# Scatters of expert outputs in two halves, and ranks dealt over 16 groups of partitions, in a hybrid SSD/attention/MoE layer

## What is computed

```
grp_logits = x @ w_rg + b_rg;  g_star = argmax(grp_logits)          # 4 groups
sel = (x @ w_re + b_re)[group g_star]                               # 8 experts in it
top_val, top_idx = top_k(sel, 2);  w2 = softmax(top_val) * p_g
expert_id = g_star * 8 + top_idx                                    # 32 experts in all
out = x + sum over the token's 2 experts of w2 * down(silu(gate(x)) * up(x))
```

## Time and profile before

| | |
|---|---|
| median of three runs | 737.94 us (736.9 to 739.18) |
| the profiled execution's own time | 737.7 us |
| its span, first to last instruction | 736.1 us |
| granted TensorE clock over the span | 0.975 |
| PE busy | 688.6 us (94%) |
| DVE, ACT, POOL busy | 384.5, 290.2, 153.3 us |
| DMA moved | 156.99 MB, mean 213 GB/s |

### The profile page before, as it was taken

How to read it: one execution, slowest core, us unless ns; L and a number is a source line. 1 busy time by engine, 2 the same in 40 slices (tenths; PEclk the granted TensorE clock), 3 DMA queues, 4 the chain that set the end, 5 groups by cost and what they waited for, 6 DMA issues and landing times.

```text
span 736.1 us, 10543 instructions
## 1 busy us (share of the span) xinstructions
PE 688.6 (94%) x3780; PEld 470.3 (64%) x3780; DVE 384.5 (52%) x850; ACT 290.2 (39%) x655; POOL 153.3 (21%) x179
## 2 busy tenths in 40 slices
PE   6999999999999999999989999989999977879984
PEld 5878788788787887666656688876543332324442
DVE  6865787876868724766787653462222211212211
ACT  5934542655455535745565432321121211112200
POOL 2300010231412101312241242001113241111321
PEclk9999999999999999999999999987999998989999
DMA  8333323333323043290020049698999999999994
GB/s 292 90 113 115 102 76 113 114 115 100 114 73 115 15 128 116 83 346 1 28 88 2 1 167 421 288 358 303 408 417 414 407 408 398 423 418 417 412 400 129
DMA packets 48454, 156.99 MB, mean 213 GB/s; under 512 B 13768, under 2 KB 13924, under 8 KB 36112
## 3 DMA queue, kind: packets, MB, share of 16 engines
q1 hardware_dynamic: 40640, 140.97, 50.2%
q0 software_dynamic: 6880, 9.02, 4.2%
q10 hardware_dynamic: 880, 6.30, 2.2%
HBM read 154.00 MB, written 18.19 MB: 234 GB/s over the span
## 4 chain that ended last, share of the span: by engine, by line
PE 70%; SPq 14%; DMA 7%; DVE 4%; issue 2%; ACT 2%; DVEq 0%; POOLq 0%; POOL 0%; ACTq 0%
PE bank L1291 14%; PE bank L1293 14%; PE bank L1292 14%; SPq L394 6%; PE bank L1672 5%; DMA s_gu<-in_w_expert_gate_dram 4%; SPq L422 4%; SPq L408 4%; PE bank L1481 3%; PE bank L1504 3%; PE bank L1490 3%; PE bank L1701 2%; PE bank L1645 2%; PE bank L1396 2%; PE bank L1629 1%
## 5 line engine op out<-in xcount | busy, mean ns | idle before, releaser
L277 DVE TENSOR_TENSOR s_wl<-s_raw,s_wh 128x512 fp32r<-128x512 f32 x105 | 89.3, 893 | 26.6 <-ACT s_wh L947 26.3
L1672 PE MATMUL bank<-s_gu,s_xgT 128*64 128x512 f32 x352 | 82.9, 626 | 17.0 <-DMA s_gu<-in_w_expert_up_dram 17.0
L947 ACT ACTIVATE s_wh<-s_raw 128x512 fp32r<-128x512 f32 x120 | 73.6, 628 | 38.5 <-PE bank L1293 18.0
L1291 PE MATMUL bank<-s_wh,s_hTh 128*128 128x512 f32 x192 | 78.9, 411 | 0.0
L1293 PE MATMUL bank<-s_wh,s_hTl 128*128 128x512 f32 x192 | 75.1, 391 | 0.0
L1292 PE MATMUL bank<-s_wl,s_hTh 128*128 128x512 f32 x192 | 74.8, 389 | 0.0
L1672 PEld LDWEIGHTS bank<-s_gu,s_xgT 128*64 128x64 f32 x352 | 27.9, 144 | 70.9 <-issue 70.9
L1213 ACT ACTIVATE s_sg<-bank,s_slot_scale 128x256 f32<-128x256 f32 x16 | 7.6, 474 | 149.5 <-PE bank L1672 112.3
L1701 PE MATMUL bank<-s_dn,s_hidT 128*64 128x512 f32 x256 | 60.4, 613 | 3.8 <-issue 1.9
L2241 DVE COPY s_hidT<-bank 128x256 f32<-128x256 f32 x16 | 6.8, 424 | 92.8 <-PE bank L1681 92.8
L2274 DVE SCALAR_TENSOR_TENSOR s_yrow<-bank,s_slot_scale,s_xg 128x512 f32<-128x512 f32 x30 | 21.1, 746 | 50.4 <-PE bank L1701 46.1
(11 more groups left out here) (303 smaller groups left out, 1402.2 us busy)
## 6 DMA issues: line engine op xcount, KB each, us to landing
s_gu<-in_w_expert_gate_dram SPq DMA_DIRECT2D x30, 1024.0 KB, 26.3
s_dn<-in_w_expert_down_dram SPq DMA_DIRECT2D x28, 1024.0 KB, 27.0
s_gu<-in_w_expert_up_dram SPq DMA_DIRECT2D x28, 1024.0 KB, 26.0
s_raw<-in_w_in_dram SPq DMA_DIRECT2D x88, 256.0 KB, 3.7
s_raw<-in_w_out_dram SPq DMA_DIRECT2D x32, 256.0 KB, 3.2
s_decay_rows<-decay_rows SPq DMA_DIRECT2D x4, 1024.0 KB, 4.7
s_xin<-in_x_dram SPq DMA_DIRECT2D x4, 512.0 KB, 5.8
s_zs<-in_x_dram SPq DMA_DIRECT2D x1, 2048.0 KB, 13.2
```

The costliest lines, as they stand in the source:

```text
L277: eng.tensor_tensor(low, full, high.bitcast(F32), ALU.subtract).then_inc(sem(f"{what}_low_{low_engine(what, i)}"), 1)
L947: act.activation(wh[:, i % HL, :], raw[:, i % RAW, :], ACT.Copy).then_inc(sem("w_high"), 1)
L1291: pe.matmul(dst, ah, bh, start=start, stop=False)
L1672: last = pe.matmul(ps[j][r, :].rearrange("p (w f) -> p w f", w=2), m["xgT"][:, j, k, r], gu[:, half, :, k, :], start=(k == 0), stop=(k == ...
```

## The change

- Each scatter of a pair p < 15 becomes two indirect DMAs, one for partitions 0 to 63 (the lower expert) and one for partitions 64 to 127 (the upper). Their semaphores count 32 a pair in place of 16. The gathers, the lone stores of L813, the gather of the last sums and the last pair's store stay whole.
- An index column is read from partition 0 on, so the upper half's indices are written once more into tables of 64 partitions (`first_far`, `second_far`, `slot_far`), by three small VectorE operations.
- TURN goes from 8 to 16: `rank_of` gives partition 4b + c the rank b + 16c (b of 16, c of 4). Sixteen consecutive ranks go to sixteen groups of four partitions.
- `turn` makes expert e start at rank 2 (e mod 8). The longest queue then ends at 56, still within 64.

```
-TURN = 8
+TURN = 16
...
+        first_far, second_far, slot_far = (sb(n, [CAP, NPAIR], I32) for n in ("first_far", "second_far", "slot_far"))
...
-            return rank_of[:, 0:CAP // 2].rearrange("p (b c) -> p c b", b=TURN)[:, 0:n // TURN, :]
+            return rank_of[:].rearrange("p (g b) -> p b g", g=TURN)[:, 0:n // TURN, :]
...
-            return 16 * sum(has_first(q) for q in range(p % 2, p + 1, 2))
+            return 32 * sum(has_first(q) for q in range(p % 2, p + 1, 2))
...
-            return 16 * sum(has_second(q) for q in range(p % 2, p + 1, 2))
+            return sum(32 if q < NPAIR - 1 else 16 for q in range(p % 2, p + 1, 2) if has_second(q))
...
-            pool.iota(rank_of[:], [[CAP // 2, 2], [1, TURN], [TURN, CAP // 2 // TURN]], ...)
+            pool.iota(rank_of[:], [[1, TURN], [TURN, CAP // TURN]], ...)
...
+            def half_rows(p, half, add):
+                near, far = (first_rows, first_far) if not add else (slot_rows, slot_far) if lone(p) else (second_rows, second_far)
+                return far[:, p:p + 1] if half else near[0:CAP, p:p + 1]
...
                 if has_first(p):
-                    pool.indirect_dma_start(out=out[:, :], ... ap=first_rows[:, p:p + 1] ..., in_=m["yrow"][:, j, :], ...)
+                    for half in range(2):
+                        r = slice(half * CAP, (half + 1) * CAP)
+                        pool.indirect_dma_start(out=out[:, :], ... ap=half_rows(p, half, False) ..., in_=m["yrow"][r, j, :], ...)
...
-                    pool.indirect_dma_start(out=out[:, :], ... ap=added_rows(p)[:, p:p + 1] ..., compute_op=ALU.add)
+                    for half in range(2):
+                        r = slice(half * CAP, (half + 1) * CAP)
+                        pool.indirect_dma_start(out=out[:, :], ... ap=half_rows(p, half, True) ..., in_=m["yrow"][r, j, :], ..., compute_op=ALU.add)
```

More of the change, by code:

```diff
@@ L663, in _ @@
                                pattern=[[1, P]], channel_multiplier=-1).then_inc(sem("consts"), 1)
-            pool.iota(rank_of[:], [[CAP // 2, 2], [1, TURN], [TURN, CAP // 2 // TURN]], base=0, channel_multiplier=0, allow_small_or_imprecise_dtypes=True)\
+            pool.iota(rank_of[:], [[1, TURN], [TURN, CAP // TURN]], base=0, channel_multiplier=0, allow_small_or_imprecise_dtypes=True)\
                 .then_inc(sem("pool_seq"), 1)
@@ L767, in _ @@
             lows(KC * 13 + HL, NSLOT)
-            pool.tensor_scalar(turn[:].rearrange("p (r v) -> p r v", v=TURN), counting(TURN).rearrange("p c b -> p (c b)").unsqueeze(1).broadcast_to([P, NE // TURN, TURN]),
-                               1.0 / P, None, ALU.mult).then_inc(sem("consts"), 1)
+            pool.tensor_scalar(turn[:].rearrange("p (r v) -> p r v", v=NEG), counting(TURN)[:, 0, 0:NEG].unsqueeze(1).broadcast_to([P, NG, NEG]),
+                               TURN / NEG / P, None, ALU.mult).then_inc(sem("consts"), 1)
             pool.wait_ge(sem("f_rstd"), TC)
@@ L832, in scatter @@
                 if has_first(p):
-                    pool.indirect_dma_start(out=out[:, :], out_offset=bass.IndirectOffsetOnAxis(ap=first_rows[:, p:p + 1], axis=0),
-                                            in_=m["yrow"][:, j, :], in_offset=None, bounds_check=T - 1, oob_is_err=False)\
-                        .then_inc(sem(f"first_out{j}"), 16)
+                    for half in range(2):
+                        r = slice(half * CAP, (half + 1) * CAP)
+                        pool.indirect_dma_start(out=out[:, :], out_offset=bass.IndirectOffsetOnAxis(ap=half_rows(p, half, False), axis=0),
+                                                in_=m["yrow"][r, j, :], in_offset=None, bounds_check=T - 1, oob_is_err=False)\
+                            .then_inc(sem(f"first_out{j}"), 16)
                 if p == NPAIR - 1:
@@ L844, in scatter @@
                     lone_landed(p)
-                    pool.indirect_dma_start(out=out[:, :], out_offset=bass.IndirectOffsetOnAxis(ap=added_rows(p)[:, p:p + 1], axis=0),
-                                            in_=m["yrow"][:, j, :], in_offset=None, bounds_check=T - 1, oob_is_err=False,
-                                            compute_op=ALU.add).then_inc(sem(f"second_out{j}"), 16)
+                    for half in range(2):
+                        r = slice(half * CAP, (half + 1) * CAP)
+                        pool.indirect_dma_start(out=out[:, :], out_offset=bass.IndirectOffsetOnAxis(ap=half_rows(p, half, True), axis=0),
+                                                in_=m["yrow"][r, j, :], in_offset=None, bounds_check=T - 1, oob_is_err=False,
+                                                compute_op=ALU.add).then_inc(sem(f"second_out{j}"), 16)
             def gather_last_sums():
@@ L2247, in rows_split @@
                 dve.tensor_scalar(first_away[:], ps[7][:, 0:NPAIR], 0.0, float(NO_ROW), ALU.is_lt, ALU.mult).then_inc(sem("dve_seq"), 1)
-                step()
-                step()
+                far = slice(CAP, 2 * CAP)
+                dve.tensor_scalar(first_far[:], ps[7][far, 0:NPAIR], float(NO_ROW), None, ALU.add).then_inc(sem("dve_seq"), 1)
+                dve.tensor_scalar(slot_far[:], ps[5][far, 0:NPAIR], float(NO_ROW), None, ALU.add).then_inc(sem("dve_seq"), 1)
+                for i in range(4):
+                    step()
+                dve.wait_ge(sem("dve_seq"), step())
+                dve.scalar_tensor_tensor(out=second_far[:], in0=ps[5][far, 0:NPAIR], scalar=float(NO_ROW), in1=first_away[far, :],
+                                         op0=ALU.add, op1=ALU.add).then_inc(sem("dve_seq"), 1)
                 dve.wait_ge(sem("dve_seq"), step())
```

## The result

The change makes the kernel slower: a median of 746.33 us (745.4 to 747.66) against 737.81 us, a ratio of 1.0119 (95% interval 1.0098 to 1.0141). The span of the profiled execution goes from 736.1 to 743.7 us.

The account below looks back on a forecast made before the run. The weight stream was taken to bound the kernel, with slow DMA engines lagging at the end. -1.3 + 0.95 - 0.5 = -0.85, + 0.1 gave about -0.8 us: 737.1 us against 737.94, range 734.8 to 740.0.

Parts of the forecast that it names:

- The bound and its place: From 575 us the weight stream limits; at the end, slow DMA engines lag by some 3.5 us from uneven rows.
- the first term of the sum: Balance of the scatters: halves spread evenly over 16 engines bring the end forward, -1.3 us, bounds 0 and -2.9.
- the sign of being wrong that I had named: At the end of the weight stream: forecast wrong if the weights' last landing moves by over 3 us.
- The fourth: Scatters: a half runs on only eight engines, slow ones lag 10 us or more, 748 us; chance 0.05.
- Rival 3: Weight stream, pairs 4 to 14: each store has its own engine price, adding 4.4 us, 741.5 us; chance 0.10.
- Rival 1: End of the kernel: balance counts in full, store landing backlog goes too, -2.7 us, 735.2 us; chance 0.19.
- Rival 2: End of the kernel: halves even nothing out, second half's later issue costs +0.95 to +1.3 us, 739.0; chance 0.18.
- What follows (VectorE, the last store, its landing) is unchanged: After the gather of the last sums: the rest of the program's end keeps its times, no cost added.
- POOL's issue: Store issue on POOL: halves take 0.65 and 1.0 us, a pair grows 1.3 us (0.6 to 3.2), hidden until pair 14.
- +0.95 - 0.5 = +0.45: Pair 14's stores to last gather: second half issued 0.95 us later, landing 0.5 us shorter with less lag.
- The small edits: VectorE's three operations, some 0.4 us before 519.7, hidden by idle time; rank tables and higher start free; completions 0.1 us.

Follow-up runs that it names:

- experiment 1: Changed kernel with halved stores kept, but the rank dealing and start ranks of the kernel before: 740.33 us, ratio 1.0043.
- experiment 2: Changed kernel with whole stores again, keeping the change's rank dealing and start ranks: 737.84 us, ratio 1.0013.
- experiment 5: Against experiment 1, halved stores kept, ranks 0 to 31 put in even partitions and 32 to 63 in odd ones: 738.01 us, ratio 1.0015.
- experiment 4: Kernel before, whole stores, with rank r put in partition r: 741.87 us, ratio 1.0063.
- experiment 10: Kernel before, whole stores, with ranks 0 to 31 in even partitions and 32 to 63 in odd ones: 741.67 us, ratio 1.0051.
- experiment 3: Against experiment 1, halved stores kept, with rank r put in partition r: 742.19 us, ratio 1.0064.

## Why the prediction was wrong

**The bound and its place: right.** The stage from 575 us is bound by the weight stream, it is the slowest engine that counts, and the lag at the end follows from the rows' spread over engines. Between the lines of the table the last weight packet moves from 724.85 to 731.25 us by where rows lie and how the stores are cut, three times what executions with unchanged stores differ by (1.9 us).

**The step that failed** is the first term of the sum: "A store of 64 partitions, with ranks dealt over 16 groups of four, gives each half's rows to all 16 engines, if the transfer is dealt in fours." The condition was not met: dealt in fours on 16 engines the change's stores would have been the evenest of all (lag 1.5), and 8.2 us were idle. A store of 64 partitions behaves as if dealt in twos, so the change's groups of four split into one engine that is much used and one that is little used. In place of -1.3 us the term measured +5.4 (731.63 against 726.26), and pair 14's rows were late by 5.7; the sign of being wrong that I had named, a last landing moved by over 3 us, came true. I had no row for a transfer of 64 partitions and took blocks of four over from those of 128; the bounds of 0 and -2.9 left out a loss, which no reason excluded. That eight engines run dry is seen, and that it takes both the halves and this dealing is shown by experiments 1 and 2. The blocks of two themselves are inferred from the four halved kernels: no record tells a packet's engine, and the same sets of partitions in another order of engines would look the same.

**The rivals.** The fourth came closest in time (748 against 746.33), with the right symptom, rows crowded on eight engines, and the wrong cause. All 16 engines are used, as the Trainium skill's page "DMA: Bandwidth & Descriptors" has it in the section "Why a DMA increments its semaphore by 16 and not by 1"; experiment 5 could not be that even on eight (1.5 us idle, where the count for eight has a lag of 16.3). Its section "The descriptor swizzle" gives the map for 128 partitions, and the whole stores of experiments 2, 4 and 10 agree roughly with it (lags of 3.3, 8.1 and 5.4 by that map, 3.1, 6.4 and 5.8 us idle); it gives none for 64. My chance of 0.05 for this rival was too low: two sections of that page of the Trainium skill pointed in different directions and nothing in the trace decided. Rival 3 fell with experiment 1: with 27 more DMAs the last down weights came 0.6 us later, within the spread of executions, where 4.4 were said. Rivals 1 and 2 were not seen.

**What the prediction left out** is POOL's drain. 27 more DMAs lengthen it by 1.5 us, and it ends the program. The step "What follows (VectorE, the last store, its landing) is unchanged" is where it should have stood. The chain of waits of the profile ends at the last DMA's issue, 730.30 + 0.72 us, 5 us before the span's end, which the source query of the last line would have shown.

**POOL's issue: the mechanism right, the size off.** A half costs nearly as much as a whole. The groups from 515 us on answer to rows 6:

```profile
L855 POOL DMA_INDIRECT out_dram<-s_yrow,s_second_rows x12 | 17.2, 1435 | 6.4 <-issue 3.3 <-DMA out_dram<-s_yrow,s_first_far 3.1
...
L841 POOL DMA_INDIRECT out_dram<-s_yrow,s_first_rows x14 | 13.1, 934 | 14.7 <-DVE s_yrow L2290 11.0 <-issue 3.7
L841 POOL DMA_INDIRECT out_dram<-s_yrow,s_first_far x14 | 12.7, 910 | 4.3 <-issue 4.3
```

That is 0.91 to 0.93 and 1.42 us, where I took 0.65 and 1.0 (a whole: 1.01 and 1.58). It was hidden as said, and the four issues at the end (722.25 to 727.83, 5.6 us) stayed within the landing: the last completion of the first stores came at 728.82. From the first store to the gather, +0.36 us was measured where +0.95 - 0.5 = +0.45 was forecast.

**The small edits** cost nothing that can be seen. With the other rank tables and the higher start but no halves the time is that of before (experiment 2). VectorE's three new operations, which that kernel does not have, took 0.17 to 0.18 us each with the change, and POOL's gather of pair 3 followed at 520.23 us, not later than the 520.59 of before.

## What to carry to other kernels

When a DMA's number of partitions changes, its map from partitions to engines may change too, so ranks dealt for one size can be the worst for another: test a dealing with the size it is meant for, and look at the DMA share at the end of a saturated stage, where a plateau at a half is the mark of half the engines idle. Splitting software DMAs is nearly free of work for the engines and costs about nine tenths of a whole issue for each half on POOL. Count POOL's DMAs over the whole program, since its last drain grows with them, and a drain put into earlier idle time takes part of that off the end.

## What was not expected of the hardware

- POOL's last drain: 5.03 us after 49 software DMAs (4.76 to 5.50 in the other kernels with 49), 6.49 to 6.51 after 76 in four of five kernels and 7.03 in the fifth (experiment 3), 3.43 us with 15 and 3.32 us with 25 since the last drain, 2.44 us with 4. As an estimate from these it is some 2.2 us and 0.055 us a DMA, but not strictly by the count. It ran past the landing of the last store in each case, by 0.1 us with 4 DMAs and by some 3 us or more with 76, so part of the 2.2 us may be no more than the wait for that landing.
- An indirect store of 64 partitions takes 0.91 to 0.93 us to issue on POOL, one of 128 takes 1.01; with adding 1.42 against 1.58 us. Most of it is fixed.
- With all 16 engines saturated, a bad spread of the stored rows (712 of 4 KB in pairs 4 to 14) is worth 5.4 us at the end of the weight stream, and the mean DMA share shows nothing of it until the fast engines run dry: it is 1.02 in the windows from 575 to 700 us of every kernel here, and with the change 0.99 from 700 and 0.84 from 710 us.
- A 4 KB row that is added in DRAM holds its engine for 327 ns, a stored or gathered one for 159 ns.
- TensorE's wait for late weights can cost twice: in experiments 4 and 10 it stood idle for 3.06 and 2.59 us, and ran the next product at a granted clock of 0.50 for a part, in 10.07 and 8.81 us in place of 7.13. It need not: in experiment 5 a wait of 2.21 us was followed by the full level (1.00).
